# The normed input in one buffer, with a chunk stride that follows the token count

## The chip, the cores and the metric

The kernel runs on one core of a Trainium2 chip. The metric is the device time of one execution in microseconds (us), as the median of several. A second measure is the span of a profiled execution, from its first to its last instruction.

## What is computed

Six layers run one after the other on 256 tokens of width 1024, in fp32: four layers of a first block, then two of a second one, for which 16 learned tokens are put in front, so that 272 tokens are held.

```python
def first_block(x, norm_w, ...):          # 256 tokens
    for i in range(4):
        hn = _rmsnorm(x, norm_w[i, 0])
        m = retention / convolution / dilated attention / retention, each with hn @ w_in ... @ w_out
        x = x + _rmsnorm(m, norm_w[i, 1])
        f = _swiglu(_rmsnorm(x, norm_w[i, 2]), ffn_w_in[i], ffn_w_out[i])
        x = x + _rmsnorm(f, norm_w[i, 3])

def second_block(h, ...):                 # 272 tokens
    for layer in range(2):
        h = h + mixer(_rmsnorm_2(h, norm_mix[layer]))       # mLSTM and RG-LRU; differential attention
        h = h + _sq_relu_mlp(_rmsnorm_2(h, norm_mlp[layer]), mlp_w1[layer], mlp_w2[layer])
    return _rmsnorm_2(h, norm_final)[:, 16:]
```

Each of the twelve norms in front of a mixer or a feed-forward layer makes a normed input, and that input is what the first product of the mixer or of the feed-forward layer multiplies. These first products are `ret_qk`, `ret_v`, `ret_g` (layers 0 and 3), `conv_in`, `att_in`, four times `ffn_in`, and in the second block `ab_xb`, `ab_gate`, `ab_qkvo`, `c_in`, two times `mlp_in`.

## The kernel before

**Layout.** Activations stand transposed: the 128 partitions hold 128 of the 1024 features, and the free dimension holds 8 chunks (`DC`) of tokens. `S1` is 256 tokens, `S2` is 272. A chunk of 256 fp32 tokens has 1024 bytes in a partition, one of 272 has 1088.

**A product in three parts.** TensorE multiplies in the type float32r, which keeps fewer bits than fp32. So both operands are split in a high part (rounded to float32r) and a low part (the rest), and `product` (lines 441 to 448) issues three matmuls for one 128 x 128 tile of weights: high weights by high input (L446), high weights by low input (L447), low weights by high input (L448). All of them add up in one PSUM bank. A unit of a product is one block of 128 outputs, mostly 8 tiles, so 24 matmuls; `multiply` waits before every fourth tile for split weights, and only in the first unit of a product for each chunk of its input.

**Weights.** SyncE loads each unit into one of four raw buffers; ScalarE rounds it (L953) and VectorE subtracts (L1408), four tiles at a time, into the buffers `weights_hi` and `weights_lo`. ScalarE and VectorE take finished banks out between these splits. The order on each engine is the order of the code; the engines meet at semaphores.

**Where the inputs of the products stand.** The normed input is in `xh` (`xn_hi` in the profile) and `xl` (`xn_lo`), each `[128, 8, 272]`, in every layer. In the 256-token layers the first 256 of a chunk's 272 places are used, so that chunks follow each other every 1088 bytes. They are written in `round_normed` (ScalarE, L1044) and in `pre_norm` (VectorE, L1441), chunk by chunk, and read by PE through `normed` and in `gates`. The second products (`ret_out`, `conv_out`, `att_out`, `ffn_out`, `ab_out`, `c_out`, `mlp_out`) read halves that stand in a large buffer (`arena_r` in the profile): every 1024 bytes in the 256-token layers, every 1088 in the others.

**Addresses.** Buffers are allocated one behind the other. In bytes within a partition, `xn_hi` begins at 64,128 and `xn_lo` at 72,832; the four `weights_hi` buffers at 39,040 and every 2,048 behind it, the `weights_lo` at 47,232 and so on; the arena at 123,712. Taken modulo 256, the weight buffers begin at 128, each arena chunk of a 256-token layer at 64, and the chunks of `xn_hi` and `xn_lo` at 128, 192, 0, 64 and so on in turn. `att_in` and `c_in` alone take weights from two further buffers in the arena, at 64 modulo 256, in every third unit.

Of the kernel before, what the change touches and what calls it, by code (L numbers as in the profile page):

```python
# [7 lines left out]
F32 = mybir.dt.float32  # L8
F32R = mybir.dt.float32r
ALU = mybir.AluOpType  # L10
ACT = mybir.ActivationFunctionType
AX = mybir.AxisListType.X

P = 128
D = 1024
DC = D // P
S1 = 256
META = 16
S2 = S1 + META
# [151 lines left out]
def build(nc, dram, out, const_at):  # L171
# [3 lines left out]
    with ExitStack() as ctx:  # L175
        def sb(name, shape):
            return ctx.enter_context(nc.sbuf_tensor(name, shape, F32))

        def sbr(name, shape):
            return ctx.enter_context(nc.sbuf_tensor(name, shape, F32R))  # L180

        def sem(name):
            return ctx.enter_context(nc.semaphore(name))
# [4 lines left out]
        w_lo = [sbr(f"weights_lo{s}", [P, SUB, P]) for s in range(SUBS)]  # L188
        h = sb("h", [P, DC, S2])
        x = h[:, :, META:S2]  # L190
        xh = sbr("xn_hi", [P, DC, S2])
        xl = sbr("xn_lo", [P, DC, S2])
        xt = sb("xn", [P, 4, S2])
        y = sb("y", [P, DC, S2])
        sq = sb("sq", [P, 4, S2])
# [21 lines left out]
        def chunks(buf, at, n, t):  # L217
            return buf[:, at:at + n * t].rearrange("p (c t) -> p c t", t=t)

        proj1 = chunks(arena, 0, 48, S1)  # L220
        proj1_r = chunks(arena_r, 0, 48, S1)
        proj2 = chunks(arena, 0, AB_IN, S2)
# [16 lines left out]
        def param(name, c=0, n=1):  # L239
            return par[:, PARAM_AT[name] + c:PARAM_AT[name] + c + n]  # L240
# [18 lines left out]
        xt_ready, xh_ready, x_split = sem("xt_ready"), sem("xh_ready"), sem("x_split")  # L259
# [181 lines left out]
        def _(pe):  # L441
            def product(acc, hi, lo, src, first, last):


                src_hi, src_lo = src
                nc.tensor.matmul(acc, hi, src_hi, start=first, stop=False)  # L446
                nc.tensor.matmul(acc, hi, src_lo, start=False, stop=False)  # L447
                return nc.tensor.matmul(acc, lo, src_hi, start=False, stop=last)  # L448
# [227 lines left out]
            def gates():  # L676

                pe.wait_ge(gates_split, 1)
                for k in range(DC):
                    pe.wait_ge(x_split, DC * (2 * DEPTH) + k + 1)  # L680
                    for gate in range(2):
                        cols = slice(gate * A_HEADS, (gate + 1) * A_HEADS)
                        last = product(PS[0:A_HEADS, 5 + gate, 0:S2], gates_hi[:, k, cols], gates_lo[:, k, cols],
                                       (xh[:, k, :], xl[:, k, :]), k == 0, k == DC - 1)
                last.then_inc(ab_sem["gate_sums"], 1)

            def mlstm(src, ready):
# [187 lines left out]

            def normed(number, n):

                return (lambda k: (xh[:, k, 0:n], xl[:, k, 0:n])), (lambda k: (x_split, DC * number + k + 1))

            def hidden(hi, lo, name):  # L880
                return (lambda k: (hi[:, k, :], lo[:, k, :])), (lambda k: (part_lo, hidden0[name] + k + 1))
# [1 line left out]
            for layer in range(DEPTH):  # L883
                norm_sum(4 * layer, S1)
                src, ready = normed(2 * layer, S1)
                if layer % 3 == 0:
                    j = layer // 3
                    dense_outputs(ph[f"ret_qk{layer}"], src, S1, ready)
                    dense_outputs(ph[f"ret_v{layer}"], src, S1, ready)
                    turn_values(j, layer)  # L890
                    dense_outputs(ph[f"ret_g{layer}"], src, S1, ready)
                    retention(j, layer)
                    dense_outputs(ph[f"ret_out{layer}"], lambda k: (ret_hi[k], ret_lo[k]), S1,
                                  lambda k: (ret_sem["split"], 4 * j + k // 4 + 1))
                elif layer % 3 == 1:
                    conv(src, ready)
                    dense_outputs(ph["conv_out"], lambda k: (conv_hi[:, k, :], conv_lo[:, k, :]), S1,
                                  lambda k: (conv_sem["split"], k + 1))
                else:
                    attention(src, ready)  # L900
                    dense_outputs(ph["att_out"], lambda k: (att_hi[:, k, :], att_lo[:, k, :]), S1,
                                  lambda k: (att_sem["mixed"], k + 2))
                post_sum(4 * layer + 1, S1)
                norm_sum(4 * layer + 2, S1)
                src, ready = normed(2 * layer + 1, S1)
                dense_pairs(ph[f"ffn_in{layer}"], src, S1, ready)
                src, ready = hidden(hid_hi, hid_lo, f"ffn_in{layer}")
                dense_outputs(ph[f"ffn_out{layer}"], src, S1, ready)
                post_sum(4 * layer + 3, S1)
            norm_sum(16, S2)  # L910
            for layer in range(2):
                src, ready = normed(2 * DEPTH + 2 * layer, S2)
                if layer == 0:
                    gates()
                    dense_outputs(ph["ab_xb"], src, S2, ready)
                    dense_outputs(ph["ab_gate"], src, S2, ready)
                    lru_gates()
                    mlstm(src, ready)
                    dense_outputs(ph["ab_out"], lambda k: (ab_hi[k], ab_lo[k]), S2,
                                  lambda k: (ab_sem["mixed"], k // 2 + 1) if k < DC else (lru_sem["done"], 1))  # L920
                else:
                    diff_attention(src, ready)
                    dense_outputs(ph["c_out"], lambda k: (c_hi[:, k, :], c_lo[:, k, :]), S2,
                                  lambda k: (c_sem["mixed"], k + 1))
                post_sum(17 + 2 * layer, S2)
                src, ready = normed(2 * DEPTH + 2 * layer + 1, S2)
                dense_outputs(ph[f"mlp_in{layer}"], src, S2, ready)
                src, ready = hidden(mlp_hi, mlp_lo, f"mlp_in{layer}")
                dense_outputs(ph[f"mlp_out{layer}"], src, S2, ready)
                post_sum(18 + 2 * layer, S2)  # L930
# [3 lines left out]
        def _(act):  # L934
# [105 lines left out]
            def round_normed(number, n):  # L1040

                for c in range(DC):
                    act.wait_ge(xt_ready, DC * number + c + 1)
                    nc.scalar.activation(xh[:, c, 0:n], xt[:, c % 4, 0:n], ACT.Copy).then_inc(xh_ready, 1)  # L1044

            def silu_pairs(phase):

# [278 lines left out]
            for layer in range(DEPTH):  # L1326
# [5 lines left out]
                else:  # L1332
                    norm(4 * layer, x, S1)
                round_normed(2 * layer, S1)
                if layer % 3 == 0:
                    j = layer // 3
# [21 lines left out]
                norm(4 * layer + 2, x, S1)  # L1358
                nc.scalar.preload_act_table(ACT.Silu)
                round_normed(2 * layer + 1, S1)  # L1360
                silu_pairs(ph[f"ffn_in{layer}"])
                exp_tables()
# [28 lines left out]
        def _(dve):  # L1391
# [43 lines left out]
            def pre_norm(k, number, src, n, weight, col):  # L1435

                dve.wait_ge(rstd_ready, k + 1)

                def rest(c):
                    dve.wait_ge(xh_ready, DC * number + c + 1)  # L1440
                    nc.vector.tensor_tensor(xl[:, c, 0:n], xt[:, c % 4, 0:n], xh[:, c, 0:n].bitcast(F32), ALU.subtract)\  # L1441
                        .then_inc(x_split, 1)

                for c in range(DC):
                    if c >= 4:
                        dve.wait_ge(x_split, DC * number + c - 3)
                    stt(xt[:, c % 4, 0:n], src[:, c, 0:n], param(weight, col + c), rstd[:, 0:n], ALU.mult, ALU.mult)\  # L1447
                        .then_inc(xt_ready, 1)
                    if c >= 2:
                        rest(c - 2)  # L1450
                rest(DC - 2)
                rest(DC - 1)
# [758 lines left out]
```

## Time and profile before

| | |
|---|---|
| median of 3 runs | 2761.72 us |
| the three runs | 2753.41, 2761.72, 2763.11 us |
| span of the profiled execution | 2749.8 us |
| PE (matmuls) busy | 2572.6 us, 94% |
| DVE (VectorE) busy | 1767.7 us, 64% |
| ACT (ScalarE) busy | 1331.8 us, 48% |
| PE's share of the chain that ended last | 87% |
| mean granted TensorE clock | 0.964 of full |

The profiled execution's own device time is not among the three; its span lies 3.6 us under the fastest and 13.3 us under the slowest of them, so about 12 us under the median. Matmuls are pipelined: one that is shown as 280 ns long is followed by the next some 115 ns later. The time from one start to the next is what adds up to the span, and below it is called the pitch. It can be read from the number of a line's matmuls between two start times: the three lines of `product` take turns, so n matmuls of one line between a first and a last start are 3(n-1) pitches.

### The profile page before, as it was taken

Reading aid. Unit: us, or ns where it says so; the run is one execution under the profiler, and the core shown is the slowest. Engines: PE = TensorE matmul, PEld = TensorE weight load, DVE = VectorE, ACT = ScalarE, POOL = GpSimd, SP = SyncE. Lnnn points to the kernel's source line nnn. Section 1 sums busy time; section 2 is a strip of 40 time slices with the busy share of each in tenths; the row PEclk is TensorE's granted clock in tenths of the full one; section 3 lists DMA queues with packets and bytes.
Section 4 is the critical chain, followed back from the end, with each engine's and each line's share of the span. In section 5 each row is a group of like instructions: output and inputs, shape, how many; then the busy total and the mean of one; then the engine's idle time right before and its main releaser. Section 6 shows DMA issues by size and latency. Waiting matters only on the chain.

```text
span 2749.8 us, 56153 instructions
## 1 busy us (share of the span) xinstructions
PE 2572.6 (94%) x19459; PEld 2454.4 (89%) x19459; DVE 1767.7 (64%) x3753; ACT 1331.8 (48%) x2781; POOL 3.4 (0%) x9
## 2 busy tenths in 40 slices
PE   7998998979999999989999999999997999887998
PEld 7988998969989999889989988998886999876998
DVE  6555666966666666666666456656576675676764
ACT  4535456544554444354554445454564444454443
POOL 0000000000000000000000000000000000000000
PEclk9999999989999999999999999999998999998999
DMA  5424553225533323325545434554232455322454
GB/s 201 167 87 145 184 197 123 92 69 168 195 133 131 109 104 107 107 92 185 199 136 183 138 120 137 193 176 154 101 122 75 149 174 176 123 92 92 156 179 131
DMA packets 103373, 385.29 MB, mean 140 GB/s; under 512 B 11344, under 2 KB 13392, under 8 KB 103024
## 3 DMA queue, kind: packets, MB, share of 16 engines
q1 hardware_dynamic: 102784, 381.90, 41.1%
q0 software_dynamic: 496, 2.24, 0.2%
q8 instruction: 47, 0.77, 0.1%
q14 instruction: 46, 0.38, 0.0%
HBM read 383.05 MB, written 1.05 MB: 140 GB/s over the span
## 4 chain that ended last, share of the span: by engine, by line
PE 87%; DVE 8%; ACT 3%; issue 1%; DMA 0%; DVEq 0%; SPq 0%; ACTq 0%
PE acc L446 25%; PE acc L448 24%; PE acc L447 24%; PE acc L492 2%; PE acc L561 2%; PE acc L617 2%; PE acc L636 1%; DVE weights_lo L1408 1%; PE acc L526 1%; PE acc L599 1%; DVE xn L1447 1%; PE acc L628 1%; PE acc L727 1%; PE acc L533 1%; PE acc L511 1%
## 5 line engine op out<-in xcount | busy, mean ns | idle before, releaser
L1408 DVE TENSOR_TENSOR weights_lo<-weights,weights_hi 128x512 fp32r<-128x512 f32 (+1 forms) x1392 | 899.4, 681 | 483.5 <-ACT weights_hi L953 477.4
L446 PE MATMUL acc<-xn_hi,weights_hi 128*128 128x256 f32 (+1 forms) x3712 | 1079.1, 291 | 49.4 <-DVE xn_lo L1441 32.7
L448 PE MATMUL acc<-xn_hi,weights_lo 128*128 128x256 f32 (+1 forms) x3712 | 1064.1, 287 | 0.0
L447 PE MATMUL acc<-xn_lo,weights_hi 128*128 128x256 f32 (+1 forms) x3712 | 1063.6, 287 | 0.0
L953 ACT ACTIVATE weights_hi<-weights 128x512 fp32r<-128x512 f32 (+1 forms) x1392 | 815.0, 621 | 224.1 <-PE acc L448 219.3
L446 PEld LDWEIGHTS acc<-xn_hi,weights_hi 128*128 128x128 f32 x3712 | 711.5, 192 | 73.3 <-issue 54.6
L448 PEld LDWEIGHTS acc<-xn_hi,weights_lo 128*128 128x128 f32 x3712 | 714.3, 192 | 0.0
L447 PEld LDWEIGHTS acc<-xn_lo,weights_hi 128*128 128x128 f32 x3712 | 711.4, 192 | 1.0
L446 PE MATMUL acc<-arena_r,weights_hi 128*128 128x256 f32 (+1 forms) x1792 | 511.1, 285 | 16.2 <-DVE weights_lo L1408 9.6
L448 PE MATMUL acc<-arena_r,weights_lo 128*128 128x256 f32 (+1 forms) x1792 | 507.6, 283 | 0.0
L447 PE MATMUL acc<-arena_r,weights_hi 128*128 128x256 f32 (+1 forms) x1792 | 506.8, 283 | 0.0
L446 PEld LDWEIGHTS acc<-arena_r,weights_hi 128*128 128x128 f32 x1792 | 340.6, 190 | 18.8 <-DVE weights_lo L1408 11.1
L447 PEld LDWEIGHTS acc<-arena_r,weights_hi 128*128 128x128 f32 x1792 | 341.2, 190 | 0.3
L448 PEld LDWEIGHTS acc<-arena_r,weights_lo 128*128 128x128 f32 x1792 | 340.2, 190 | 0.0
L1052 ACT ACTIVATE silu<-acc 128x256 f32<-128x256 f32 x88 | 33.9, 385 | 190.2 <-PE acc L448 190.2
L982 ACT ACTIVATE arena<-acc 128x256 f32 (+2 forms) x112 | 43.3, 386 | 170.5 <-PE acc L448 170.5
L1468 DVE TENSOR_TENSOR sum_of_squares<-sum_of_squares,sq 128x256 f32<-128x256 f32 (+1 forms) x96 | 41.3, 431 | 84.0 <-ACT sq L999 63.4
L492 PE MATMUL acc<-sq,const_a 128*128 128x256 f32 (+1 forms) x144 | 54.7, 551 | 33.6 <-ACT sq L1030 33.4
L1146 ACT ACTIVATE arena<-acc 128x256 f32<-128x256 f32 x72 | 27.4, 380 | 114.6 <-PE acc L448 114.6
L492 PEld LDWEIGHTS acc<-sq,const_a 128*128 128x128 f32 x144 | 39.1, 283 | 48.7 <-ACT sq L1030 29.8
L1503 DVE TENSOR_TENSOR arena_r<-arena,arena_r 128x256 f32 (+3 forms) x152 | 65.8, 433 | 21.0 <-DVE arena_r L1501 2.2
L446 PE MATMUL acc<-xn_hi,arena_r 128*128 128x256 f32 (+1 forms) x256 | 75.8, 296 | 0.0
(262 smaller groups left out, 2357.0 us busy)
## 6 DMA issues: line engine op xcount, KB each, us to landing
weights<-in_ffn_in SPq DMA_DIRECT2D x176, 512.0 KB, 3.2
weights<-in_ffn_out SPq DMA_DIRECT2D x64, 704.0 KB, 4.0
weights<-in_att_in SPq DMA_DIRECT2D x72, 512.0 KB, 3.2
weights<-in_mlp_in SPq DMA_DIRECT2D x64, 512.0 KB, 3.2
weights<-in_mlp_out SPq DMA_DIRECT2D x64, 512.0 KB, 3.3
weights<-in_ret_qk SPq DMA_DIRECT2D x32, 512.0 KB, 3.2
weights<-in_ret_v SPq DMA_DIRECT2D x32, 512.0 KB, 3.2
weights<-in_ret_g SPq DMA_DIRECT2D x32, 512.0 KB, 3.2
```

The source lines that it names most:

```text
L446: nc.tensor.matmul(acc, hi, src_hi, start=first, stop=False)
L447: nc.tensor.matmul(acc, hi, src_lo, start=False, stop=False)
L448: return nc.tensor.matmul(acc, lo, src_hi, start=False, stop=last)
L492: nc.tensor.matmul(PS[:, 4, 0:n], mean, sq[:, c % 4, 0:n], start=(c == 0), stop=(c == DC - 1))\
L561: last = nc.tensor.matmul(PS[:, 4 + parity, 0:S1], conv_diag[:, parity * PE_TAPS + t, :], conv_u[:, m, t:t + S1], start=(t == 0), stop=(t ...
L617: last = nc.tensor.matmul(PS[:, 2 + 2 * (u % 2) + g // 2, (g % 2) * S1:(g % 2 + 1) * S1], att_q[rows, g, it * P:(it + 1) * P], att_k[rows, ...
L953: nc.scalar.activation(w_hi[sub % phase.subs][:, 0:n, :], raw[slot][:, j * SUB:j * SUB + n, :], ACT.Copy)\
L982: nc.scalar.activation(dst[:, i * phase.body + u, 0:n], PS[:, u % SLOTS, 0:n], func).then_inc(out_evacuated, 1)
L1052: nc.scalar.activation(silu[:, u // 2, 0:S1], PS[:, u, 0:S1], ACT.Silu).then_inc(gate_ready, 1)
L1408: nc.vector.tensor_tensor(w_lo[sub % phase.subs][:, 0:n, :], raw[slot][:, j * SUB:j * SUB + n, :], w_hi[sub % phase.subs][:, 0:n, :].bitca ...
L1468: nc.vector.tensor_tensor(ssum[:, 0:n], ssum[:, 0:n], sq[:, o, 0:n], ALU.add).then_inc(y_added, 1)
L1503: nc.vector.tensor_tensor(lo, t, hi.bitcast(F32), ALU.subtract).then_inc(part_lo, 1)
```

## The change

The two buffers become one, `xn_parts`, of the same total size and in the same place (64,128 on). Two pairs of views are laid on it. For 272 tokens, both halves stand where they stood. For 256 tokens, chunks follow each other every 256 tokens (1024 bytes), and the low half begins behind the eight chunks of the high one, 8,192 bytes on. Every chunk of the 256-token layers, high or low, then begins at 128 modulo 256. No other buffer moves; each engine has the same instructions, waits and DMAs in the same order, with other addresses in some.

```diff
-        xh = sbr("xn_hi", [P, DC, S2])
-        xl = sbr("xn_lo", [P, DC, S2])
+        xn_parts = sbr("xn_parts", [P, 2 * DC * S2])
...
+        xn_hi = {S1: chunks(xn_parts, 0, DC, S1), S2: chunks(xn_parts, 0, DC, S2)}
+        xn_lo = {S1: chunks(xn_parts, DC * S1, DC, S1), S2: chunks(xn_parts, DC * S2, DC, S2)}
...
-                                       (xh[:, k, :], xl[:, k, :]), k == 0, k == DC - 1)
+                                       (xn_hi[S2][:, k, :], xn_lo[S2][:, k, :]), k == 0, k == DC - 1)
...
-                return (lambda k: (xh[:, k, 0:n], xl[:, k, 0:n])), (lambda k: (x_split, DC * number + k + 1))
+                return (lambda k: (xn_hi[n][:, k, :], xn_lo[n][:, k, :])), (lambda k: (x_split, DC * number + k + 1))
...
-                    nc.scalar.activation(xh[:, c, 0:n], xt[:, c % 4, 0:n], ACT.Copy).then_inc(xh_ready, 1)
+                    nc.scalar.activation(xn_hi[n][:, c, :], xt[:, c % 4, 0:n], ACT.Copy).then_inc(xh_ready, 1)
...
-                    nc.vector.tensor_tensor(xl[:, c, 0:n], xt[:, c % 4, 0:n], xh[:, c, 0:n].bitcast(F32), ALU.subtract)\
+                    nc.vector.tensor_tensor(xn_lo[n][:, c, :], xt[:, c % 4, 0:n], xn_hi[n][:, c, :].bitcast(F32), ALU.subtract)\
```

## Rows read from the trace of the kernel before

**Rows 1.** The page: span, busy time by engine, the last chain by engine.
```profile
span 2749.8 us, 56153 instructions
PE 2572.6 (94%) x19459; PEld 2454.4 (89%) x19459; DVE 1767.7 (64%) x3753; ACT 1331.8 (48%) x2781; POOL 3.4 (0%) x9
PE 87%; DVE 8%; ACT 3%; issue 1%; DMA 0%; DVEq 0%; SPq 0%; ACTq 0%
```

**Rows 2.** Waits, longest in total first: who waited for whom, us, times, longest.
```profile
DVE weights_lo L1408 <- ACT weights_hi L953: 477.4, 500, 13.2
ACT weights_hi L953 <- PE acc L448: 219.3, 316, 1.1
ACT silu L1052 <- PE acc L448: 190.2, 88, 2.2
```

**Rows 3.** Groups by line and shape: count | busy us, mean ns | idle before.
```profile
L447 PE MATMUL acc<-xn_lo,weights_hi 128*128 128x256 f32 x2688 | 765.9, 285 | 0.0
L447 PE MATMUL acc<-xn_lo,arena_r 128*128 128x256 f32 x192 | 53.9, 281 | 0.0
L447 PE MATMUL acc<-arena_r,weights_hi 128*128 128x256 f32 x1088 | 303.4, 279 | 0.0
L447 PE MATMUL acc<-xn_lo,weights_hi 128*128 128x272 f32 x1024 | 297.6, 291 | 0.0
L447 PE MATMUL acc<-arena_r,weights_hi 128*128 128x272 f32 x704 | 203.4, 289 | 0.0
```

**Rows 4.** One line in ffn_in0: duration min/median/max ns, first and last start.
```profile
L447 PE MATMUL acc<-xn_lo,weights_hi x305: 279/282/283, 271.8 to 379.7; 128*128 128x256 f32 x153
```

**Rows 5.** The same line in ffn_out0.
```profile
L447 PE MATMUL acc<-arena_r,weights_hi x119: 276/276/276, 399.8 to 439.9; 128*128 128x256 f32 x119
```

**Rows 6.** The same line in att_out.
```profile
L447 PE MATMUL acc<-arena_r,weights_hi x55: 276/276/280, 1185.9 to 1204.3; 128*128 128x256 f32 x55
```

**Rows 7.** The same line in conv_out.
```profile
L447 PE MATMUL acc<-arena_r,weights_hi x56: 281/281/281, 584.8 to 604.2; 128*128 128x256 f32 x56
```

**Rows 8.** With 272 tokens: L447 in mlp_out0, and L446 in the gates (4 weight columns).
```profile
L447 PE MATMUL acc<-arena_r,weights_hi x106: 282/288/292, 2290.0 to 2329.8; 128*128 128x272 f32 x106
L446 PE MATMUL acc<-xn_hi,w_gates_hi x16: 283/287/292, 1864.2 to 1869.8; 128*4 128x272 f32 x16
```

**Rows 9.** The same line at half clock, in ffn_in3 and in ret_out3.
```profile
L447 PE MATMUL acc<-xn_lo,weights_hi x7: 415/416/420, 1663.7 to 1667.9; 128*128 128x256 f32 x7
L447 PE MATMUL acc<-arena_r,weights_hi x3: 415/415/415, 1608.1 to 1609.4; 128*128 128x256 f32 x3
```

**Rows 10.** Stretches (ffn_in0, ffn_out0, att_in, conv_in): busy by engine, granted clock, DMA share, GB/s.
```profile
core 0: us, PE busy (x) PEld busy (x) DVE busy (x) ACT busy (x) POOL busy (x), PEclk, DMA share, GB/s
262.00:388.00 126.00, 125.89 (x1049) 125.61 (x1050) 82.59 (x160) 61.17 (x115) 0.00 (x0) 0.99 0.54 184
819.00:1162.00 343.00, 338.79 (x2552) 318.54 (x2552) 218.16 (x609) 147.87 (x333) 0.00 (x0) 0.99 0.32 110
461.00:549.00 88.00, 84.69 (x543) 79.79 (x544) 81.91 (x190) 52.29 (x145) 0.00 (x0) 0.95 0.27 90
...
394.00:434.00 40.00, 40.00 (x355) 40.00 (x355) 22.89 (x38) 22.10 (x45) 0.00 (x0) 1.00 0.58 195
```

**Rows 11.** Timeline of PE in att_out behind a pause: start us, us.
```profile
1185.66 0.39 PE L446 MATMUL acc<-arena_r,weights_hi 128*128 128x256 f32 x1
1185.88 0.28 PE L447 MATMUL acc<-arena_r,weights_hi 128*128 128x256 f32 x1
1186.00 0.28 PE L448 MATMUL acc<-arena_r,weights_lo 128*128 128x256 f32 x1
1186.12 0.28 PE L446 MATMUL acc<-arena_r,weights_hi 128*128 128x256 f32 x1
1186.23 0.28 PE L447 MATMUL acc<-arena_r,weights_hi 128*128 128x256 f32 x1
```

**Rows 12.** The writer of the low half, and a VectorE subtraction into chunks 1024 bytes apart.
```profile
L1441 DVE TENSOR_TENSOR xn_lo<-xn,xn_hi 128x256 fp32r<-128x256 f32 x64 | 25.4, 417 | 1.8 <-ACT xn_hi L1044 1.8
L1503 DVE TENSOR_TENSOR arena_r<-arena,arena_r 128x256 f32 x80 | 34.0, 426 | 11.4
```

## The prediction

> **What bounds the kernel now.** I read the page first. PE is busy 94% of the span, and 87% of the chain that ended last is PE's [rows 1]. Then the waits: the longest are of DVE for ACT and of ACT for PE [rows 2]. DVE and ACT wait for PE to free buffers and finish banks, and PE itself has next to no idle time ahead of the product lines [rows 3]. In a feed-forward product PE is busy 125.9 of 126 us, DVE 82.6 and ACT 61.2 [rows 10]. So the kernel is as long as its row of matmuls, and the pitch, the time from one start to the next, is what to look at.
>
> The change touches nothing but addresses, so the question is whether an address can alter the pitch. The trace holds the comparison. In ffn_in0 the input comes from `xn_hi` and `xn_lo`, chunks 1088 bytes apart: 305 matmuls of L447 from 271.8 to 379.7, which is 107.9 us / (304 x 3) = 118.3 ns [rows 4]. In ffn_out0 input of the same shape comes from the arena, chunks 1024 bytes apart: 40.1 / (118 x 3) = 113.3 ns [rows 5]. In att_out it is 18.4 / (54 x 3) = 113.6 ns [rows 6]. The durations say the same, 282 against 276 ns, and in the fast stretches they hardly vary, which contention with DVE or ACT would not give. Which buffer is read is not the reason: with 272 tokens both are 1088 bytes apart, and there the means of both buffers are near each other, 291 and 289 ns [rows 3].
>
> So a stretch in which every chunk starts at the same place modulo 1024 can run at 113.4 ns, where the same work with a start that wanders 64 bytes from chunk to chunk takes 118.3. The fast pitch does not set in at once. Behind a pause in att_out the starts follow after 220, 120, 120 and 110 ns [rows 11], so the gain needs some four matmuls alike; before the change the place moves every three.
>
> There is one row against it, and it matters. conv_out reads the arena too, with 1024 bytes from chunk to chunk and its low half 8,192 bytes behind the high one, which is what the change makes of the normed input. It runs at 19.4 / (55 x 3) = 117.6 ns, every one of 56 durations 281 ns [rows 7]. att_out, with the same two distances, is fast. So equal places permit the fast pitch and do not force it: of eight second products of the 256-token layers seven are fast (two ret_out, four ffn_out, att_out) and one is not. I read that as two steady patterns, of which a stretch falls into one when it starts.
>
> **The change part by part.**
> *The 256-token first products.* L446 to L448 have 3 x (2,688 + 192) = 8,640 matmuls on the normed input with 256 tokens [rows 3]. At half clock nothing is to be had: 416 ns there from `xn_lo`, 415 from the arena [rows 9]. Half clock covers some 50 us of these products, by the granted clock of their stretches; at a pitch of 213 ns (256 columns at 1.2 GHz) that is some 235 matmuls. That leaves 8,405. If all go from 118.3 to 113.4, the gain is 8,405 x 4.9 = 41 us; if all behave like conv_out, 8,405 x 0.7 = 6 us. If the new places suit worse, it is a loss, priced below.
>
> *What it loses on the way.* The fast pattern must be found again behind each pause. att_in has 72 units with other matmuls between many of them. By the starts of rows 11 the first four cost about 13 ns more than four at 113.4: 72 x 13 ns = 1 us. In att_in PE is busy 338.8 of 343 us, with DVE at 218 [rows 10], so a shorter row of matmuls shows there nearly in full; I take 1 us off for waits that move to ScalarE's copies. conv_in is the tightest place: PE 84.7, DVE 81.9 of 88 us [rows 10]. Its 384 matmuls could give 1.9 us; I count 1. Together 3 us: 41 - 3 = 38 us.
>
> *What could be late next.* In ffn_in0 DVE has 43 us of 126 to spare, ACT 65, so a product that is 4% shorter meets neither. The weights must arrive faster: 184 GB/s x 118.3 / 113.4 = 192 GB/s, and ffn_out0 takes 195 GB/s with the DMA engines at 0.58 and PE at 40.00 of 40 us [rows 10]. That cover holds.
>
> *The writers.* ACT and DVE write the two halves at new distances. A subtraction into chunks 1024 bytes apart is 426 ns, the present one 417 [rows 12]: 64 x 9 ns = 0.6 us at most, and most of that lies ahead of chunks that PE doesn't yet need. I count nothing.
>
> *The 272-token layers.* Both halves stand where they stood; zero.
>
> Sum: the gain of 38 us is against the profiled execution: 2749.8 - 38 = 2711.8 us of span. What lies around the span stays, so against the median 2761.7 - 38 = 2724 us.
>
> **The rivals.**
> *A, nearly all first products find the fast pattern: 2724 us.* For it: seven of eight stretches with equal places, and that it takes hold within some four matmuls. Against it: in all seven the input starts at 64 modulo 256 and the weights at 128. With the change the input starts at 128, as the weights do. No row shows that pair for more than three matmuls in a row.
>
> *B, some do.* A stretch that starts badly stays slow to its end, as conv_out's 24 tiles and more did. With half of the 8,405 in the fast pattern the gain is about 20 us: 2742 us.
>
> *C, none does: 2756 us.* All run like conv_out, 117.6 ns, or stay at 118.3 because the pair of places rules the fast pattern out. The gain is 0 to 6 us: 2756 to 2762 [rows 4, 7]. That the change does nothing at all belongs here too.
> The Trainium skill would put it here for another reason. TensorE: Matmul & The Clock Gate, section "Wait — 56ns, not 53.3ns?", gives the start-to-start time of warm matmuls as N / 2.4 GHz plus about 2.5 ns, with no part for the address. By that rule the sum would be zero and the pitch 109.2 ns before and after. The trace does not agree: 113.3, 117.6 and 118.3 ns at one N.
>
> *D, slower: 2790 us.* The weights of the next matmul are read while the input of the present one is. Now they begin 64 bytes apart in turn (0, 64, 128, 192), so that a meeting at one place is passed by the next chunk. With the change they always begin at the same place modulo 256, and the meeting may recur in each matmul. One step of 64 bytes, 16 columns at 2.4 GHz, is 6.7 ns. Once in two matmuls that is 8,405 x 3.35 = 28 us on top: 2790; once in each, 56 us: 2818. It decides at a mean pitch of 118.3 + 1.7 = 120.0 ns (14 us / 8,405). For it: conv_out shows that equal places can be held in a slow pattern. Against it: with 272 tokens the gates, with four weight columns to load and so hardly any reading of weights, run at 5.6 / 45 = 124.4 ns, and full weights in mlp_out0 at 39.8 / 315 = 126.3 [rows 8]. The reading of weights costs 2 ns there, so little of the excess over the columns' own time is a quarrel with weights. That also speaks for A, since the place against the weights then matters little.
>
> **How the numbers follow.** A 0.53, B 0.17, C 0.19, D 0.11. The likeliest is A: 2724 us, its own range 2714 to 2733, given by 35 to 41 us of gain and the 8 us by which the fastest run of before lies under the median. The range of 8 in 10 reaches from A's lower end through B and C to no change: 2712 to 2764. D and a bit beyond A's end are left out. A change of under 0.5% (13.8 us) is about what a measurement of this kernel cannot tell from none. Faster by more: A and nearly all of B, 0.69. Within: C and the slow end of B, 0.20. Slower: D, 0.11.
>
> **What the profile after would show.** A: in ffn_in0 the durations of L447 on the normed input are 276 ns flat and its pitch 113.4, and each ffn_in takes 122 us in place of 127.5. B: whole stretches at 276 and others at 281. C: 281 or the mixed 279 to 283. D: durations above 284. In each case the 272-token products stay at 282 to 292 ns, and the second products, conv_out with its 281, are as they were, unless their start moves them into the other pattern, which would be worth 192 x 4.2 ns = 0.8 us for conv_out, or cost up to 528 x 4.3 = 2.3 us for one ffn_out. The forecast is wrong if ffn_in has 276 ns and the span still doesn't fall: then PE wasn't the bound, and waits for DVE or for weights would stand ahead of L446.

## The result: 0.6% slower

Against the kernel before, run beside it, the changed kernel takes 2770.8 us in the median (2766.9 to 2773.1) where the other takes 2757.6 (2752.8 to 2763.1): a ratio of 1.0057, with a 95% interval of 1.0036 to 1.0078 (the quotient of the two medians alone is 1.0048, inside it). The profiled execution's span grew from 2749.8 to 2771.3 us, by 21.5 us. The forecast was 2724 us and a range of 2712 to 2764.

The profile after, in the order of the forecast. First the page (span, busy by engine, the last chain by engine), to be laid beside rows 1:

```profile
span 2771.3 us, 56153 instructions
PE 2593.5 (94%) x19459; PEld 2472.3 (89%) x19459; DVE 1768.9 (64%) x3753; ACT 1332.3 (48%) x2781; POOL 3.4 (0%) x9
PE 88%; DVE 7%; ACT 3%; issue 1%; DMA 0%; DVEq 0%; ACTq 0%; SPq 0%
```

PE's busy time grew by 20.9 us; DVE's and ACT's grew by about 1 us and 0.5 us. The bound is where it was, and it became longer. The lines of `product` are now L447 to L449, and the middle one, which was L447, is L448. Its groups by shape, as rows 3:

```profile
L448 PE MATMUL acc<-xn_parts,weights_hi 128*128 128x256 f32 x2688 | 767.6, 286 | 0.0
L448 PE MATMUL acc<-arena_r,weights_hi 128*128 128x256 f32 x1088 | 305.7, 281 | 0.0
L448 PE MATMUL acc<-xn_parts,weights_hi 128*128 128x272 f32 x1024 | 297.4, 290 | 0.0
L448 PE MATMUL acc<-xn_parts,arena_r 128*128 128x256 f32 x192 | 53.5, 279 | 0.0
```

The normed input with 256 tokens went from 285 to 286 ns, and the second products, whose addresses did not change, from 279 to 281. Line by line (duration min/median/max, first and last start), ffn_in0, ffn_out0, ffn_out2, conv_out and mlp_out0 after the change, as rows 4, 5, 7 and 8:

```profile
L448 PE MATMUL acc<-xn_parts,weights_hi x301: 283/283/283, 271.7 to 379.7; 128*128 128x256 f32 x151
L448 PE MATMUL acc<-arena_r,weights_hi x118: 276/276/276, 401.0 to 440.8; 128*128 128x256 f32 x118
L448 PE MATMUL acc<-arena_r,weights_hi x125: 281/281/281, 1376.0 to 1419.8; 128*128 128x256 f32 x125
L448 PE MATMUL acc<-arena_r,weights_hi x43: 276/276/420, 587.7 to 604.8; 128*128 128x256 f32 x43
L448 PE MATMUL acc<-arena_r,weights_hi x107: 282/290/292, 2299.7 to 2339.9; 128*128 128x272 f32 x107
```

ffn_in0 is now as even as the forecast wanted it, every duration the same, but at 283 ns, not at 276: its pitch is 108.0 / (300 x 3) = 120.0 ns. Every other first product of the 256-token layers whose weights stand in their own buffers runs at 119.6 to 120.3 ns as well, mostly at 120.0. Among the second products three have changed sides: conv_out is fast now, and ret_out0 and ffn_out2 are slow, the latter at 43.8 / (124 x 3) = 117.7 ns.

A third thing grew. The stretch that is called the tail of the attention below lies between the last product matmul of att_in and the first of att_out. Busy time, granted clock and DMA share in it, before:

```profile
core 0: us, PE busy (x) PEld busy (x) DVE busy (x) ACT busy (x) POOL busy (x), PEclk, DMA share, GB/s
1162.00:1182.00 20.00, 15.63 (x104) 13.01 (x102) 12.53 (x49) 6.51 (x18) 0.00 (x0) 1.00 0.08 27
```

and after:

```profile
1171.50:1200.50 29.00, 25.16 (x105) 21.25 (x104) 14.22 (x51) 7.10 (x18) 0.00 (x0) 0.62 0.06 19
```

The same hundred matmuls of the attention took 29 us in place of 20, at a granted clock of 0.62 in place of 1.00. The sums of the stretches, from the first to the last start of each product, in us. Starts were read to 0.1 us, so a sum can be off by one or two tenths. The 272-token layers are counted from the first matmul of the gates on. The two columns "again" are second profiles of the two kernels, of which more below.

| | before | after | before again | after again |
|---|---|---|---|---|
| first products, 256 tokens | 1221.1 | 1231.9 | 1220.8 | 1230.2 |
| second products, 256 tokens | 387.5 | 392.6 | 388.6 | 388.6 |
| attention's tail | 20.7 | 29.3 | 30.1 | 29.3 |
| what lies between and ahead of those products | 234.9 | 233.2 | 236.9 | 232.3 |
| the 272-token layers | 876.1 | 874.8 | 876.1 | 875.2 |
| to the last product matmul | 2740.3 | 2761.8 | 2752.5 | 2755.6 |

So of the 21.5 us half is in the first products (10.8), 5.1 in the second ones and 8.6 in the tail; the rest gives 3 back. The 5.1 us are ret_out0 (2.8), ffn_out2 (2.3) and att_out (1.9, because the tail's low clock reaches into its first unit), less 0.7 in conv_out and 1.3 in ret_out3.

### The profile page after: what moved, and what is told of

Same layout as the page of the kernel before. It is cut to its first block, busy times and chain, and to the rows that moved or that the text cites. A ratio compares the mean times of both kernels' runs of the same rounds, so it can differ in the third digit from the quotient of the medians.

```text
span 2771.3 us, 56153 instructions
## 1 busy us (share of the span) xinstructions
PE 2593.5 (94%) x19459; PEld 2472.3 (89%) x19459; DVE 1768.9 (64%) x3753; ACT 1332.3 (48%) x2781; POOL 3.4 (0%) x9
## 4 chain that ended last, share of the span: by engine, by line
PE 88%; DVE 7%; ACT 3%; issue 1%; DMA 0%; DVEq 0%; ACTq 0%; SPq 0%
PE acc L447 25%; PE acc L449 24%; PE acc L448 24%; PE acc L493 2%; PE acc L618 2%; PE acc L637 2%; PE acc L562 2%; PE acc L527 1%; PE acc L629 1%; DVE xn L1448 1%; DVE weights_lo L1409 1%; PE acc L600 1%; PE acc L728 1%; PE acc L534 1%; PE acc L512 1%
## 5 line engine op out<-in xcount | busy, mean ns | idle before, releaser
L447 PE MATMUL acc<-xn_parts,weights_hi 128*128 128x256 f32 (+1 forms) x3712 | 1085.0, 292 | 51.0 <-DVE xn_parts L1442 32.7
L449 PE MATMUL acc<-xn_parts,weights_lo 128*128 128x256 f32 (+1 forms) x3712 | 1065.8, 287 | 0.0
L448 PE MATMUL acc<-xn_parts,weights_hi 128*128 128x256 f32 (+1 forms) x3712 | 1064.9, 287 | 0.0
L447 PEld LDWEIGHTS acc<-xn_parts,weights_hi 128*128 128x128 f32 x3712 | 715.2, 193 | 76.9 <-issue 54.6
L448 PEld LDWEIGHTS acc<-xn_parts,weights_hi 128*128 128x128 f32 x3712 | 717.8, 193 | 1.0
L449 PEld LDWEIGHTS acc<-xn_parts,weights_lo 128*128 128x128 f32 x3712 | 717.0, 193 | 0.0
L447 PE MATMUL acc<-arena_r,weights_hi 128*128 128x256 f32 (+1 forms) x1792 | 513.5, 287 | 15.3 <-DVE weights_lo L1409 9.5
L449 PE MATMUL acc<-arena_r,weights_lo 128*128 128x256 f32 (+1 forms) x1792 | 510.1, 285 | 0.0
L448 PE MATMUL acc<-arena_r,weights_hi 128*128 128x256 f32 (+1 forms) x1792 | 509.7, 284 | 0.0
L447 PEld LDWEIGHTS acc<-arena_r,weights_hi 128*128 128x128 f32 x1792 | 342.0, 191 | 17.7 <-DVE weights_lo L1409 10.7
L449 PEld LDWEIGHTS acc<-arena_r,weights_lo 128*128 128x128 f32 x1792 | 343.0, 191 | 0.0
L448 PEld LDWEIGHTS acc<-arena_r,weights_hi 128*128 128x128 f32 x1792 | 342.4, 191 | 0.3
L493 PEld LDWEIGHTS acc<-sq,const_a 128*128 128x128 f32 x144 | 37.8, 276 | 48.6 <-ACT sq L1031 30.1
L1515 DVE TENSOR_TENSOR arena<-acc,silu 128x256 f32<-128x256 f32 x88 | 37.4, 426 | 63.1 <-PE acc L449 63.1
```

The lines of the kernel that those rows point to most:

```text
L493: nc.tensor.matmul(PS[:, 4, 0:n], mean, sq[:, c % 4, 0:n], start=(c == 0), stop=(c == DC - 1))\
```

## The experiments

They ask four things. Is it the place of the input against that of the weights that sets the pitch? What settles which of two patterns a stretch falls into? Whose is the tail? And is there a place that beats both kernels? Below, "pair" is the input's place less the weights' place, modulo 256 bytes. The change made it 0 for all 256-token first products with weights in their own buffers, and the arena's chunks have 192 against those buffers. All kernels but the repeats are the changed kernel with the edit shown.

### The pair, moved from the input's side

```diff
-        xn_hi = {S1: chunks(xn_parts, 0, DC, S1), ...
-        xn_lo = {S1: chunks(xn_parts, DC * S1, DC, S1), ...
+        xn_hi = {S1: chunks(xn_parts, n, DC, S1), ...              # n = 16, 32, 48 floats
+        xn_lo = {S1: chunks(xn_parts, n + DC * S1, DC, S1), ...
```

> The changed kernel with both halves of the 256-token input 64 bytes further on, at 192 modulo 256, so 64 bytes past the weights' place (128). Nothing else moves. Theory P (what counts is the input's place less the weights' place, modulo 256): this is the pair that att_in's every third unit has in the changed kernel, so the pitch is 117.4 ns in all first products but those units of att_in, and the time is (120.0 - 117.4) x 8,000 = about 21 us under the changed kernel, 2750 us. Rival Q (what counts is the buffer, its distance between the halves, or anything that a shift of 64 bytes leaves): 120.0 ns and 2771 us.

> Both halves of the 256-token input 128 bytes further on, at 0 modulo 256, 128 past the weights' place. No stretch of either trace has this pair for long. Theory P says only that the pitch is one steady value or two, flat along a unit, and not necessarily 120; by the 272-token rows, where the pairs 0 and 128 are alike, 120 ns and 2771 us. Rival Q: 120.0 ns and 2771 us as well. Together with the other two shifts it gives the table of pitch by pair.

> Both halves of the 256-token input 192 bytes further on, at 64 modulo 256, the place of the arena's chunks: 64 bytes before the weights' place (192 past it). Theory P: the first products behave like the second ones, 113.3 ns in stretches that start well and 117.7 in others; att_in's every third unit (arena weights, pair 0) gives 120. With three quarters of the stretches fast: 2771 - 8,000 x 5.5 ns = 2727 us; all slow: 2752 us. Rival Q: 120.0 ns and 2771 us.

Measured: pair 64 gives 2759.3 us (ratio 1.0016, 1.0004 to 1.0028), pair 128 gives 2764.5 (1.0034, 1.0023 to 1.0046), pair 192 gives 2735.3 (0.9939, 0.9924 to 0.9954). The theory that the pair counts had expected 2750, about 2771 and 2727 us: the order is as expected, the sizes are not (pair 64 runs at 117.8 ns and not at 117.4, pair 128 has two values, and at pair 192 more stretches were slow). The rival, 2771 us for all three, is out. The middle line in ffn_in0 at pairs 64, 128 and 192, and for the last also in ffn_in1:

```profile
L448 PE MATMUL acc<-xn_parts,weights_hi x306: 278/279/280, 272.0 to 379.8; 128*128 128x256 f32 x153
L448 PE MATMUL acc<-xn_parts,weights_hi x301: 281/281/281, 271.7 to 379.7; 128*128 128x256 f32 x151
L448 PE MATMUL acc<-xn_parts,weights_hi x307: 281/281/281, 271.7 to 379.8; 128*128 128x256 f32 x154
L448 PE MATMUL acc<-xn_parts,weights_hi x118: 276/276/276, 700.1 to 739.8; 128*128 128x256 f32 x118
```

These are pitches of 117.8, 120.0 and 117.8 ns, and 39.7 / (117 x 3) = 113.1. At pair 64 all first products are at 117.8, but for four units of conv_in and one of att_in at 113.4; at pair 128 a stretch is at 118.7 or 120.0; at pair 192 it is at 113.4 or 117.8, just the two values that the arena's products show. In att_in and conv_in, where pauses part the units, single units differ: at pair 192, 17 of att_in's 48 units with weights in their own buffers are at 117.8 and 30 at 113.4. In att_in of the last kernel every third unit takes its weights from the arena, so with pair 0, among units with pair 192:

```profile
L448 PE MATMUL acc<-xn_parts,weights_hi x352: 276/276/281, 834.1 to 1149.2; 128*128 128x256 f32 x176
L448 PE MATMUL acc<-xn_parts,arena_r x177: 280/283/283, 830.4 to 1149.8; 128*128 128x256 f32 x177
```

One input, one stretch, two places of weights: 276 and 283 ns in the median. So the 283 ns of the changed kernel's ffn_in is what pair 0 gives here too.

### The pair, moved from the weights' side

The weight buffers go 192 bytes up (64 modulo 256), and what lies behind keeps its place modulo 256. The arena's products, whose inputs stay where they were, get pair 0; the first products get pair 64.

```diff
+        sb("pad_before", [P, 48])
         w_hi = [sbr(f"weights_hi{s}", ...
...
+        sb("pad_after", [P, 16])
         h = sb("h", [P, DC, S2])
...
-        N_ARENA = 26400
+        N_ARENA = 26336
```

> The changed kernel with only the split weight buffers (weights_hi, weights_lo) 64 bytes back, at 64 modulo 256; the normed input stays at 128, the arena and all else keep their places modulo 256. Theory P (the pair counts): the first products become the pair 64 and go from 120.0 to 117.8 ns; the second products of the 256-token layers, whose inputs do not move, become the pair 0 and go from 113.3 or 117.7 to 120.0 ns; att_in's every third unit, whose weights are in the arena, stays at 117.4. Rival U (the input's own place counts, the weights' does not): first products 120.0, second products 113.3 or 117.7, as in the changed kernel.

Measured: 2772.2 us, in one execution. The middle line (L450 here) in ffn_in0 and in ffn_out0:

```profile
L450 PE MATMUL acc<-xn_parts,weights_hi x307: 279/279/279, 271.8 to 379.9; 128*128 128x256 f32 x154
L450 PE MATMUL acc<-arena_r,weights_hi x110: 283/283/283, 402.7 to 442.0; 128*128 128x256 f32 x110
```

All eight second products run at 120.0 ns and together take 407.6 us where the changed kernel's took 392.6; the first products of the ret, conv and ffn layers run at 117.8 as with the input moved. So the same pair made in two ways gives the same pitch there, and the input's place alone doesn't. One expectation was missed: att_in's units with arena weights, at pair 64, have a mean of 115.0 ns, not 117.4, since 15 of 24 are at 113.4 and the others at 117.8. Its units with weights in their own buffers mix the two as well (23 of 48 at 113.4), where with the input moved one of 48 did. So pair 64 has the fast pattern too, if only among pauses, and what favours it there is open.

### What settles the pattern at pair 192

The kernel with pair 192 once more, nothing changed.

> The kernel of in_plus192 once more, for a second profile of one and the same program. Theory S (which of the two patterns, 113.3 or 117.7 ns, a stretch of the pair 192 falls into is settled by nanoseconds at its start, which differ from execution to execution): another set of stretches is slow than in the first profile (there ret_out0, ffn_in0, ffn_out0, ret_qk3, ret_out3, ffn_in3, ffn_out3), and the spans differ by several us. Rival T (the program's own addresses settle it): the same seven stretches are slow, and the span is within 2 us of 2742.

Measured: 2726.1 us, in one execution. ffn_in0, slow the first time (281 ns), is fast:

```profile
L448 PE MATMUL acc<-xn_parts,weights_hi x303: 276/276/276, 272.0 to 374.7; 128*128 128x256 f32 x152
```

Slow are ret_v0 and ret_qk3, and conv_in and att_in mix as before (conv_in has 116.3 ns, in the first profile 116.0); all other first and second products are fast, while in the first profile seven were slow throughout. The first products took 1187.4 us, against 1195.3 in the other execution, and the second ones 389.1 against 396.1. So the pattern can differ from execution to execution, and a stretch without pauses keeps the one with which it starts. What settles it at the start is not shown.

### Steps between, and the 272-token products

In the 272-token layers the chunk stride of 1,088 bytes makes every place wander. In the MLP's second products it can be 1,280 (five times 256), so that all chunks have one place. The first kernel does that alone, at pair 192; the others take pairs 0, 64 and 128 there, and for the normed input the pairs 208, 176 and 224 around the good one.

```diff
-        mlp_hi, mlp_lo = chunks(arena_r, 0, MLP, S2), chunks(arena_r, MLP * S2, MLP, S2)
+        mlp_hi, mlp_lo = (chunks(arena_r, m + n * MLP * 320, MLP, 320)[:, :, 0:S2] for n in range(2))
```

(In this edit n is 0 for the high half and 1 for the low one. The four kernels have m = 0, 16, 32, 48 floats, and 0, 52, 44, 56 floats as the n of the first edit.)

> The changed kernel, with the hidden halves of the two MLPs of the second block 1280 bytes apart instead of 1088, so that all their chunks of 272 tokens begin at 64 modulo 256. Theory P with equal places as the only condition: mlp_out0 and mlp_out1 (1,536 matmuls, 126.1 ns now) go to 113.3 x 272 / 256 = 120.4 ns, 9 us less, 2762 us. Rival R (the fast pattern also needs a length of whole 256 bytes, so that one read ends where the next begins): 124 to 126 ns as in the gates, where six matmuls in a row have one place, and a gain of 0 to 3 us.

> 256-token input at 80 modulo 256, so 208 past the weights' place, 16 bytes beyond the pair 192; MLP hidden halves 1280 bytes apart at 128 modulo 256, the pair 0. If the meeting of the two reads is graded in 16 bytes, the first products keep two patterns with somewhat other values (between 113 and 118) and perhaps one only; if only the 64-byte step counts, they equal pair 192 (113.3 and 117.7) or pair 208's neighbour 0 (120). For the MLP the pair 0 should cost more than the 123.3 ns of pair 192, about 125 to 127.

> 256-token input at 48 modulo 256, the pair 176, 16 bytes short of 192; MLP hidden halves 1280 bytes apart at 192 modulo 256, the pair 64. Graded in 16 bytes: values between pair 192 (113.3, 117.7) and pair 128 (118.7, 120.0). MLP: between 122 and 126 ns.

> 256-token input at 96 modulo 256, the pair 224, half way from 192 to 0; MLP hidden halves 1280 bytes apart at 0 modulo 256, the pair 128. Graded: between 113.3 to 117.7 and 120.0 ns, so about 117 to 119 and a time near the kernel before. If 224 still behaves like 192, the fast pattern has a range of places. MLP: between 123 and 127 ns.

Measured: 2765.1, 2762.6, 2765.4 and 2767.7 us. The middle line in mlp_out0 of the first:

```profile
L448 PE MATMUL acc<-arena_r,weights_hi x109: 285/285/288, 2290.0 to 2330.0; 128*128 128x272 f32 x109
```

Pair 192 gives 123.3 ns there against 126.1 with the wandering stride, 2.0 us for each of two products. Expected, if equal places were all it needs, were 120.4 ns and 9 us. Pairs 0, 64 and 128 give 125.4, 126.7 and 126.7: the order of the pairs is another than with 256 tokens, but 192 is the best in both. The normed input at 176, 208 and 224 runs at about 119.3, 119.2 and 118.3 ns (ret_qk0 alone is at 116.6 at 208). For 208 some value from 113 to 118 or 120 had been expected, so that was missed. The good place is narrow: 16 bytes beside it nearly all is lost.

### Can the two halves stand better apart?

Pair 192 for the high half, and 0 or 128 for the low one.

```diff
-        xn_lo = {S1: chunks(xn_parts, 48 + DC * S1, DC, S1), ...
+        xn_lo = {S1: chunks(xn_parts, 48 + d + DC * S1, DC, S1), ...    # d = 16, 48 floats
```

> in_plus192 with the low half of the 256-token input 64 bytes further (pair 0), the high half at pair 192. One matmul in three reads the low half. If each matmul is priced by its own pair: L448 at 120.0 ns and the other two at 113.3 to 117.7, mean 115.5 to 118.5. If the order of pairs along the row counts instead, all three differ from that; a mean under 115.4 would be the better layout.

> in_plus192 with the low half of the 256-token input at pair 128, the high half at pair 192. Priced by its own pair: L448 at 118.7 to 120.0 ns and the other two at 113.3 to 117.7, mean 115.1 to 118.5. A mean under 115.4 in all stretches would be a layout without the slow pattern.

Measured: 2764.4 and 2762.4 us, one execution each. In neither does any stretch of first products on the weight buffers reach 113.4; they lie between 117.8 and 119.4. Nor is each matmul priced by its own pair: in ffn_in0 with the low half at pair 0, the line that reads it (L448) has 281 ns in the median, and the two that read the high half have 284 and 282. With the high half at pair 192, the fast pattern was seen only where the low half stands there too; two other places of the low half were tried, in one profile each.

### Whose is the tail?

Both kernels once more, and the changed one in more executions.

> The kernel before, a second profile of it. If the full clock in the attention's tail of its first profile is one of two ways in which this same program runs, this profile may show the tail (from att_in's last product to att_out's first) at 28 to 30 us and half clock, with a time near 2763 us; if the half clock belongs to the change, the tail is at 20.6 us again, with a time near 2753 us. A time near 2753 us with a tail of 28 to 30 us would say that the tail has nothing to do with the two groups of times. The first products' mean pitch should be 118.3 ns again either way.

> The changed kernel, a second profile of it. First products at 120.0 ns throughout in either theory. If the second products' pitch is settled in each execution, other stretches than ret_out0 and ffn_out2 run at 117.6 ns this time; if it is settled by the program, the same two do. If the tail's clock differs between executions, it may be at 20 us here; if it belongs to the change it is at 29 us again.

> The changed kernel again, in more rounds, nothing left out. The executions of the kernel before lie in two groups, 2751 to 2755 and 2761 to 2765 us, and two profiles of it put the 9.4 us between them into the attention's tail. If the changed kernel has both groups too, some of its executions lie near 2757 us and the others at 2766 to 2773 us; if the change has shut it out of the lower group, all lie at 2766 to 2773 us. Its products give 2766 us with every second product at 113.3 ns and 2771 us with two of them at 117.7 ns.

Measured: before again 2763.8 us, span 2762.0; after again 2766.9, span 2765.1, one execution each. The second products of after again are all fast, ret_out0 and ffn_out2 too. The tails of the two:

```profile
1164.00:1193.50 29.50, 25.66 (x104) 21.73 (x103) 14.17 (x51) 6.95 (x18) 0.00 (x0) 0.58 0.06 19
```

```profile
1165.50:1194.00 28.50, 24.83 (x103) 21.11 (x103) 14.01 (x50) 6.82 (x18) 0.00 (x0) 0.61 0.06 19
```

The same program, before the change, has the tail at a granted clock of 1.00 in one execution and 0.58 in another, and is 9.4 us longer in it. That is the gap between two groups in which its executions lie: of 68 that ran beside the experiments, 44 are at 2750.9 to 2755.4 us and 24 at 2761.1 to 2765.2. The changed kernel has no such pair of groups. Ten executions of it, five of them from the last run (2768.7 us, ratio 1.0056, 1.0042 to 1.0069), all lie between 2766.6 and 2773.1, and its three profiles have the tail at 29.2 to 29.3 us. So the long tail is a way in which the kernel before can run too, but the changed kernel was never seen in the better one. Set group against group, the median of the ten (2768.8 us) lies 5.6 us above the upper group of the kernel before (2763.3) and 16.2 above the lower (2752.6): of the 0.6% some 0.2% is left where the tails are alike.

The same holds for every other kernel here. All sixteen profiles but the first of before have a tail of 28.4 to 30.1 us, so the ratios of the experiments hold it too. With pair 64 the first products took 1215.5 us, less than the 1221.1 of before, and yet the ratio is 1.0016. The kernel with pair 208 seems to have a lower group (four of ten executions at 2749.7 to 2756.4). No profile shows it there, and why an address should decide over the clock behind 340 us of att_in is open.

The two again profiles, alike in the tail and in the second products, also show what the first products cost by themselves: 9.4 us. Of these the span kept 3.1, since what lies between the products was 4.6 us shorter after the change, the tail 0.8 and the 272-token layers 0.9. The mean granted clock is 0.956 before again and 0.963 after again. Within the first products both profiles of before have the half clock for 50 us (213 and 210 matmuls), and the three of the changed kernel for 38 to 39 us (161 to 164 matmuls). A matmul at half clock takes 213 ns and one at full clock 120, so that is 49 x 0.093 = 4.6 us which the changed kernel got back. Why it has less of the half clock is open.

conv_out in the second profile of before shows another point, that the pattern can differ between executions of that kernel too. Rows 7 have 56 durations of 281 ns; the same program gave

```profile
L447 PE MATMUL acc<-arena_r,weights_hi x56: 276/276/371, 585.1 to 604.7; 128*128 128x256 f32 x56
```

### A version that beats both

Pair 192 for the normed input and for the MLP's halves, the first edit with n = 48 and the fourth with m = 0.

> The changed kernel with the 256-token views of the normed input 192 bytes further on (its places at 64 bytes above a multiple of 256, the weights' at 128) and the two halves of the gated product at a chunk stride of 1,280 bytes, every chunk at 64 as well; nothing left out. If the place of the input against the weights' sets the pitch, the gains of the two single edits add up: first and second products between 113.3 and 117.9 ns, the MLP's second products at about 123.3 ns, so 4 us below the kernel with the first edit alone: about 2731 us, a ratio of 0.992, with executions apart by up to 20 us as the stretches fall into the one or the other pattern. If the two edits have nothing to do with each other but their gains depend on the executions caught, the ratio is anywhere from 0.990 to 0.998.

Measured: 2733.7 us (2719.3 to 2740.9), a ratio of 0.991 with an interval of 0.9884 to 0.9936, near the 2731 us and 0.992 that were expected. The MLP's second products in it:

```profile
L448 PE MATMUL acc<-arena_r,weights_hi x163: 285/288/288, 2269.8 to 2329.8; 128*128 128x272 f32 x163
```

They take 94.9 and 95.1 us in place of 96.9 and 97.1. The intervals of this kernel and of the one with the first edit alone overlap, so that the second edit pays is shown by its stretches and not by the medians. The executions lie up to 21.6 us apart. In the profiled one, of 2740.9 us, four first and four second products are slow throughout.

## Why the prediction was wrong

**The bound** was read rightly: PE's row of matmuls, and within it the pitch. No wait took its place. (The rows cited for PE's idle time, rows 3, show the middle line alone, which never waits; the first line, L446, sat idle for 49.4 us ahead of its matmuls on the normed input and for 16.2 us ahead of those on the arena, 2% of the span together.) DVE and ACT kept their times, the writers too (L1442 on 256 tokens is 419 ns, before 417 [rows 12], where I allowed up to 426), and the weights arrived in time.

**The step that failed** is "a stretch in which every chunk starts at the same place modulo 1024 can run at 113.4 ns, where the same work with a start that wanders 64 bytes from chunk to chunk takes 118.3" [rows 4 to 6]. The gain of 38 us was that step times 8,405 matmuls; the part itself is a loss of 10.8 us in the profiled execution. The two rows differ in two things: whether the place wanders, and which place it is against the weights. I gave the difference to the first. The runs show that holding a place is not enough, and that the pair decides. Held places yield, with the weight buffers at 128:

| pair | 0 | 64 | 128 | 192 |
|---|---|---|---|---|
| pitch, ns | 120.0 | 117.8 (113.4 in some units of att_in and conv_in) | 118.7 or 120.0 | 113.4 or 117.8 |

The wandering stride, which visits all four in turn, shows 118.3 ns, a value among them. It is not made up of them: in the kernel before, the tiles at the pairs 0, 64, 128 and 192 take 118.1, 117.6, 118.5 and 119.1 ns per matmul (from the starts in ret_qk, ret_v, ret_g and ffn_in at full clock, 490 tiles each; the second profile gives the same within 0.1). A tile at pair 0 among others does not cost the 120.0 of the held one, and a tile at pair 192 gets nothing of the 113.4. So three matmuls in a row at pair 192 do not bring the fast pattern. It needs a held place, as the prediction had it, and the right one as well. The change put the 256-token inputs for good at the worst pair, 1.7 ns above what wandering gave. The objection stood in the prediction, under rival A: "No row shows that pair for more than three matmuls in a row." It ought to have weighed more than the seven fast stretches, which were seven times the same pair.

The profile after has none of the four signs that were named. 283 ns flat is neither C's 281, nor its mix of 279 to 283, nor D's "durations above 284"; by its pitch of 120.0 it stands just where D was said to begin.

**D** had the right condition, weights and input that begin at the same place modulo 256 in each matmul, and the right sign for it; that the reads collide there is its picture, which no run shows. Its price, one step of 6.7 ns once in one or two matmuls, was wrong. Measured are 120.0 - 118.3 = 1.7 ns. Over 8,405 matmuls that is 14 us, and 10.8 us are seen (9.4 in the second pair of profiles). The 4.6 us that came back from the half clock are about the difference; in att_in, which grew by only 0.3 us, the half clock covers 3.4 us after the change and 6.3 before. The argument against D from the gates, in which little of the excess went away with four weight columns [rows 8], compared rows whose place wanders over all pairs, and couldn't show what a single pair does.

**conv_out** [rows 7] was read as "two steady patterns, of which a stretch falls into one when it starts". That held, and goes further than I took it: the side can differ between executions of one program. The forecast gave at most 2.3 us to one ffn_out that moves to the slow side. Measured were 2.3 us there and 2.8 us in ret_out0 (52.4 for 49.6 us); conv_out's gain of 0.7 us was foreseen as 0.8. In the second profile of after both are fast, so nothing says that this part of the first comparison belongs to the change.

**The clock of the tail** was in no term; it was put at nothing, since the span of before was taken as it stood, and it is 8.6 of the 21.5 us. The page of before gives one execution, which was one of the lower group. I set the gain against that span and then against a median 12 us above it, and named the distance, but didn't ask which stretch holds it. A look at the three runs (2753, 2762, 2763) would have given the question.

**Two sums** don't come out, and neither changes the outcome. By the four starts of rows 11 (220, 120, 120, 110) the first four steps cost 116 ns more than four at 113.4; the 13 ns leave out the first step. And 35 to 41 us of gain with 8 us below give 2713 to 2727 for A, not 2714 to 2733.

**The rule that case C cites**, N / 2.4 GHz plus about 2.5 ns (the Trainium skill, TensorE: Matmul & The Clock Gate, "Wait — 56ns, not 53.3ns?"), has no part for the address and would have given no change. For N = 256 the traces show 113.4 to 120.0 ns by the pair, and not 109.2; the measurement decides, and the address has a part in it.

## What to carry to other kernels

Where PE is the bound, look at a product's pitch with the start of its input less the start of its weights, modulo 256 bytes, and try the four places before any stride: here the best of them gave a ratio of 0.994 against the wandering stride and the worst 1.006, both with the tail's long form in them. The wandering stride lay between the best and the worst held place, with 256 columns and with 272, so a regular stride is a gain or a loss by where it starts. And before a sum is made against a span, look whether the runs fall into groups, and take the second profile that tells which stretch is the difference.

## What the runs showed of the hardware

- The pitch of float32r matmuls (128 x 128 weights, 256 columns, full clock) depended on the pair of places: from 113.4 to 120.0 ns, and with 272 columns from 123.3 to 126.7. It did so whichever side was moved. A place that wanders gave 118.3 and 126.1 ns; with 256 columns its tiles don't have the values of the held pairs. Why 192 is the good pair is open; no run here shows what reads collide.
- Some pairs have two steady patterns with the same instructions and addresses (276 and 281 ns shown at pair 192). A stretch without pauses keeps the one it has fallen into, ffn_in through its 1,056 matmuls, and another execution may take the other; behind a pause, as in att_in and conv_in, it can change.
- A stretch of 20 us with small matmuls and pauses had a granted clock of 1.00 in one execution and 0.58 in another of the same program, which is 9.4 us.
